# TensorE runs products with unread results in the seven pauses in which a norm's vector is made

## The reference

```python
def rmsnorm(x, g):
    return x * lax.rsqrt(jnp.mean(x * x, axis=-1, keepdims=True) + EPS) * g
h = modulate(rmsnorm(x, norm_g[l, 0]), sh1, s1)          # h * (1 + scale) + shift
# block 1, layer 0: y = even_mixer(h, hc, ...)           (norms x0 and ctx)
# block 1, layer 1: y = conformer_conv(h, ...)           (norm conv; inside it the layer norm ln)
x = x + g1 * y
x = x + g2 * sq_relu_mlp(modulate(rmsnorm(x, norm_g[l, 1]), sh2, s2), w_ff1[l], w_ff2[l])   # mlp0, mlp1
x = rmsnorm(x, final_g)                                  # fin
# block 2: mixer on the norm b2, then PEER (each token gathers 128 expert rows) on the norm ffn
```

## Time and profile before

| | |
|---|---|
| median of 3 executions | 1623.35 us (1622.1 to 1623.39) |
| profiled execution | 1622.0 us, span 1620.7 us |
| TensorE busy | 1392.3 us (86%) |
| VectorE busy | 1212.4 us (75%) |
| ScalarE busy | 728.9 us (45%) |
| GpSimd busy | 349.2 us (22%) |
| mean granted TensorE clock | 0.958 of full speed |
| HBM traffic | 294 GB/s over the span |

### The profile page before, as it was taken

How to read it: one execution, slowest core, us unless ns; L and a number is a source line. 1 busy time by engine, 2 the same in 40 slices (tenths; PEclk the granted TensorE clock), 3 DMA queues, 4 the chain that set the end, 5 groups by cost and what they waited for, 6 DMA issues and landing times.

```text
span 1620.7 us, 20626 instructions
## 1 busy us (share of the span) xinstructions
PE 1392.3 (86%) x7504; PEld 1033.9 (64%) x7504; DVE 1212.4 (75%) x2373; ACT 728.9 (45%) x1636; POOL 349.2 (22%) x313
## 2 busy tenths in 40 slices
PE   7999889999897899998999779988787777777776
PEld 3777789999887899997878756643232232222232
DVE  6966778887997688876866697877777787777654
ACT  4455265555567655554344444433333333333322
POOL 1100010001000100002001135464454444444430
PEclk8999899999999999997999889999999999999999
DMA  9742459998520489993523369999999999999994
GB/s 390 314 185 79 155 177 345 337 338 311 192 95 1 156 329 337 340 340 109 186 100 105 117 244 408 420 419 420 420 420 421 420 421 420 421 420 420 420 420 204
DMA packets 66056, 477.15 MB, mean 294 GB/s; under 512 B 7330, under 2 KB 7330, under 8 KB 8738
## 3 DMA queue, kind: packets, MB, share of 16 engines
q0 software_dynamic: 36864, 268.45, 40.0%
q1 hardware_dynamic: 29088, 207.37, 34.6%
q10 hardware_dynamic: 2, 0.01, 0.0%
HBM read 474.75 MB, written 1.05 MB: 294 GB/s over the span
## 4 chain that ended last, share of the span: by engine, by line
PE 45%; DMA 28%; DVE 19%; ACT 4%; issue 3%; POOL 2%; SPq 0%; POOLq 0%; ACTq 0%; DVEq 0%
DMA row_h<-in_uv,crow 21%; PE ps L1960 6%; PE ps L1565 5%; PE ps L1566 5%; PE ps L1567 5%; DMA row_x<-in_uv,crow 5%; DVE HID L794 4%; PE ps L1846 4%; PE ps L1845 4%; PE ps L1843 4%; DVE WB L473 3%; ACT WB L1083 1%; PE ps L1605 1%; PE ps L1607 1%; PE ps L1606 1%
## 5 line engine op out<-in xcount | busy, mean ns | idle before, releaser
L473 DVE TENSOR_TENSOR WB<-ring,WB 128x1024 fp32r<-128x1024 f32 x232 | 287.2, 1238 | 98.3 <-ACT WB L1083 94.7
L1083 ACT ACTIVATE WB<-ring 128x1024 fp32r<-128x1024 f32 x232 | 243.4, 1051 | 128.7 <-PE ps L1846 85.1
L1565 PE MATMUL ps<-hH,WB 128*128 128x256 f32 x920 | 267.9, 291 | 4.8 <-DVE WB L473 3.2
L1960 PE MATMUL ps<-ring,P 128*128 128x512 f32 x448 | 211.2, 616 | 65.7 <-ACT P L1413 64.3
L1566 PE MATMUL ps<-hL,WB 128*128 128x256 f32 x920 | 261.1, 284 | 0.0
L1567 PE MATMUL ps<-hH,WB 128*128 128x256 f32 x920 | 261.0, 284 | 0.0
L1960 PEld LDWEIGHTS ps<-ring,P 128*128 128x128 f32 x448 | 83.3, 195 | 187.6 <-ACT P L1413 99.8
L1403 ACT ACTIVATE On<-On 128x2 f32<-128x2 f32 x128 | 26.0, 203 | 380.7 <-DVE On L1017 380.6
L1017 DVE CUSTOM_DVE_ANT_0 ring<-ring,cT 128x1024 f32<-128x1024 f32 x112 | 136.2, 1225 | 76.5 <-DMA ring<-in_uv,crow 75.6
L1565 PEld LDWEIGHTS ps<-hH,WB 128*128 128x128 f32 x920 | 177.3, 193 | 9.9 <-issue 5.1
L1566 PEld LDWEIGHTS ps<-hL,WB 128*128 128x128 f32 x920 | 177.4, 193 | 2.2 <-issue 2.2
(11 more groups left out here) (293 smaller groups left out, 2733.1 us busy)
## 6 DMA issues: line engine op xcount, KB each, us to landing
ring<-in_stream SPq DMA_DIRECT2D x116, 1024.0 KB, 5.8
ring<-in_um SPq DMA_DIRECT2D x66, 1024.0 KB, 7.2
ring<-in_wm SPq DMA_DIRECT2D x4, 1024.0 KB, 12.9
bias<-in_bias SPq DMA_DIRECT2D x2, 2048.0 KB, 16.0
HID<-in_um SPq DMA_DIRECT2D x4, 512.0 KB, 18.0
ring<-in_uv,crow POOLq DMA_INDIRECT x112, 28.4
xT<-in_xT SPq DMA_DIRECT2D x1, 1024.0 KB, 8.9
cT<-in_cxT SPq DMA_DIRECT2D x1, 1024.0 KB, 14.5
```

The lines of the kernel that those rows point to most:

```text
L473: ve.tensor_tensor(unit_dst(j, 1), unit_src(j), f(unit_dst(j, 0)), ALU.subtract).then_inc(s_lo, 1)
L1083: se.activation(unit_dst(j, 0), unit_src(j), ACT.Copy).then_inc(s_hi, 1)
L1565: te.matmul(o, wh[:, c], hi[:, kt, :], start=(kt == 0), stop=False)
L1960: mm = te.matmul(ps[4 + 2 * n + q][:, :], diag[:, g % 8, :], row_ap[row_of[g]][:, 1024 + q * 512:1536 + q * 512], start=(g % 128 == 0), st ...
```

## The change

A helper `stand_in` issues n products of the float32 constant `ones` with a source of 512 columns, each with start and stop set, into a bank that nobody reads until it has been written anew. It is called seven times, each time between the last product ahead of the pause and the first wait of `rows2`. Only the call at mlp0 brings a wait of its own, for the DMA of `bsp`, which is long over.

```diff
+            def stand_in(bank, src, n):
+
+                for _ in range(n):
+                    te.matmul(bank[:, :], ones[:], src, start=True, stop=True)
...
             m0.then_inc(mm, "c")
+            stand_in(ps[2], xT[:, 0:2, :], 7)
             rows2(0, [("w_in", 2, 0, 0), ("w_in", 2, 1, 0)], normed("x0"), (hH, hL))
...
             mean_of_sum("mlp0")
+            T.wait_ge(s_bsp, 16)
+            stand_in(ps[3], bsp[:], 6)
...
             mean_of_sum("conv")
+            stand_in(ps[3], bsp[:], 6)
             rows2(first["pw1", 0], [("pw1", 0, 0, 0), ("pw1", 0, 1, 0)], normed("conv"), (hH, hL))
...
                 mean_square("ln", kt)
+            stand_in(ps[3], bsp[:], 6)
...
             mean_of_sum("mlp1")
+            stand_in(ps[3], bsp[:], 6)
             mlp(1)
             mean_of_sum("b2")
+            stand_in(ps[3], bsp[:], 6)
...
             mean_of_sum("ffn")
+            stand_in(ps[3], bsp[:], 7)
```

## The result

The changed kernel takes 1613.18 us (median of 5, 1612.78 to 1615.58) where the kernel before takes 1623.35 us. The medians lie 10.2 us apart. The ratio of the runs, which comes with an interval and is used for comparisons from here on, is 0.9944 (95% interval 0.9933 to 0.9955), or 9.1 us (7.3 to 10.9).

What follows compares the result with a forecast made beforehand. TensorE was taken as bound by half-clock products behind seven norm pauses. Five net gains, 5.5 us, less 1.0 for seams and 0.2 for the wait behind b2, gave 4.3: 1623.35 to 1619.0 us, range 1615.5 to 1622.5.

Steps and rivals of the forecast that it cites:

- the five places: mlp0, conv, ln, mlp1 and ffn: full clock in rows2 less delay gains 1.7, 0.5, 1.2, 1.2 and 0.9 us.
- The sum of 5.5 us: Gains less delays at mlp0, conv, ln, mlp1 and ffn, passed on to the end: 5.5 us before deductions.
- The seams: Two changes between groups of different products at each of five places, 0.1 us taken for each: 1.0 us lost.
- Two of the seven give nothing: At b2 and x0 other engines' work sets what follows, so an earlier end of rows2 gains 0 us.
- The argument about the third unit: Behind b2: it waits for VectorE's split, then GpSimd's sum of fin; neither depends on rows2, so no gain.
- the longer wait: Behind b2: a 2.3 us wait may cost the clock, between 0 and 1.5 us; 0.2 us taken as loss.
- A lost clock: Rival, all pauses: products of a constant don't hold the clock, 14 us or more lost, about 1637 us; chance 0.05.
- The delay: Rival: stand-ins 0.6 to 1.0 us too long at each place eat the gain, 1620.3 to 1624 us; chance 0.24.
- More than the sum: Rival: cold stretches on average as long as at mlp0, and fewer seams: 7.4 us gained, 1616 us; chance 0.11.
- The x0 case: At x0: no gain; the clock may fall at 30.3 under the stand-ins, taken as nothing, 2.5 us kept for range.

Runs made afterwards that it cites:

- experiment 10's kernel with products around fin: Changed kernel without its call at b2, but with one product of ones ahead of the mean of fin and one behind it: 1616.34 us, ratio 0.9964.
- the second run of experiment 9: Changed kernel with each call one product shorter, stand-ins in eight smaller pauses and nine products ahead of the first mix: 1602.67 us, ratio 0.9875 to the kernel before.

## Why the prediction was wrong

**The clock and the five places: right.** The clock is held at all seven, and inside their stages the five places won 1.75, 0.56, 1.27, 1.29 and 1.02 us where the terms were 1.7, 0.5, 1.2, 1.2 and 0.9. The sum of 5.5 us stands at 5.9 in every profile with these calls; the timed run of the five agrees within its wide interval (5.2 to 9.6). Some luck is in it: the same stages of the second profile of the kernel before are together 1.1 us longer, and a forecast from that profile would have had other terms (conv's alone differs by 1.4).

**The seams: mis-sized.** "Between nothing and 0.2 us each, I take 0.1, so 1.0 us": they cost nothing. At mlp0 the last stand-in record starts at 216.24, 0.02 us before the first `rows2` product, and the second `rows2` product starts at 216.78, 0.54 us behind the stand-in. That is one stand-in record at its pitch of 0.43 and one of `rows2` at 0.12, with nothing between them. The first record of `rows2` only looks longer (0.68 us). So `rows2` takes 6.04 us from the first start to the last, and not 5.7, and begins 4.97 us after the start of the mean's last product instead of 4.53, 0.44 us late instead of 0.84. The two deviations cancel. This term, 1.0 us on the losing side, is the first part of the miss.

**"Two of the seven give nothing", and the clock elsewhere: wrong for b2, right for x0.** This is the step that failed. The argument about the third unit holds: it starts at the same place of the work with the call and without. The clock was lost behind the longer wait (747.3 to 750.7), which the prediction had named as a sign of being wrong and priced at 0.2 us; it costs 1.3 us in the third unit, of which 0.45 are left when the column products start. What was left out is that the clock's other slow stretches are not fixed. The sum counted the clock only directly behind each pause and put the change in all other slow stretches at nothing, without a reason. The kernel before has 13.6 us of them behind fin, at nearly the same place in three profiles. The call at b2 alone turns them into 6.8 us and is worth 4.2 us; two products around fin shorten them as much.

In the whole change the same stretch is 10.2 us long and 1.1 us are won there. This is not the call's doing: the two kernels that have the earlier calls but not b2's have 10.2 us there too and win 1.6. So the effect of b2 alone can't be added to that of the five. What the call does in the change, its profiles show between 775 and 915 us: 1.1 us are won, and both kernels without the call lose 2.9 to 3.1 there. Their profiles are the slowest of their five runs, and the timed difference is smaller, 1.6 us.

**The rest.** Put together, the profiles have 5.8 us at the five places, 1.1 behind fin, 1.1 up to 915 us and 0.95 between 932 and 1078 us. The second profile of the kernel before is itself 0.95 us quicker in that last part than the first, so it is chance between executions, and I don't count it as a gain of the change. The other 8.0 stand against the 4.3 of the forecast.

**A misread row.** The granted clock in the earlier trace rows is 8 or 7 tenths in slices 0, 4, 18, 22 and 23, counted from 0; a 9 stands for 90% or more. The prediction lists other slices. Nothing in its sum was worked out from them.

**The rivals.** A lost clock did not come; the run with tiny products shows its price, +1.2%. The delay (0.44 us at mlp0) didn't eat the gain; one product fewer wins back 0.35 us a place in a profile. "More than the sum" was what happened, but for another reason than the one it was given: the slow stretches directly behind the five pauses were not longer than forecast, others became shorter. The x0 case was as forecast: no gain, and no fall of the clock at 30.3 in the changed kernel's profile.

**What stays open.** Why the five earlier calls alone shorten the stretch behind fin from 13.6 to 10.2 us, and why the call at b2 goes with a missing slow stretch near 890 us. All six profiles with a call of six products at b2 and the later waits unfilled are without the 10.2 us there and win 1.1 us up to 915 us; the seven without the call (the kernel before and its edits among them) have the 10.2 us in four and not in three, and so has the kernel with five products at b2. A stretch that comes and goes between executions is thus mixed with what the call does, and one profile for each kernel doesn't separate them. Nor do the single runs: they spread over 2 to 9 us without clear groups, except for experiment 10's kernel with products around fin (one at 1609.53, four from 1615.0 on).

## What to carry to other kernels

Where TensorE waits some 4 us for a short chain and the granted clock reads 0.50 behind the wait, products with unread results in the wait paid 0.44 of the slow stretch, less what they overran, in each of five places (at ln the norm capped the gain). Full products did it and products of 2 columns did not. One product too few won a little more than one too many in the profile; in the time that isn't shown. Before counting, list every slow stretch of the profile and not only those behind the pauses that are edited: filling one pause was worth up to 4 us at another. A forecast made from one profile should allow for that with a term of both signs, since stretches also differed between executions of unedited work by up to 3 us. The kernel with the most pauses filled (the second run of experiment 9) gained the most, within 1.8 us over four runs.

## What I had not expected of the hardware

The clock falls while TensorE is busy for 3.40 of 3.40 us with products of 2 rows and 2 columns, and in the kernel before it stays down through the 8.7 us that are left of the products 128 rows deep and 4 columns wide behind fin (757.4 to 766.1). And the place where it falls can repeat: in three profiles, of kernels that differ only at x0, the 13.6 us behind fin began within 0.5 us of the same product, while near 890 us the same three had 3.4 us twice and 10.2 us once.
